# Scale and shift of the first two feature blocks computed by 128 columns at a time, with the token tiles loaded first

## The reference, cut to what matters

```python
c_act = jax.nn.silu(c)                                # (1, 1024)
mod = jnp.dot(c_act, w_ada[l]) + b_ada[l]             # (1, 6 * 1024)
sh_m, sc_m, g_m, sh_f, sc_f, g_f = jnp.split(mod, 6, axis=-1)
h = modulate(rmsnorm(x, norm_mix_g[l]), sh_m, sc_m)   # x_hat * g * (1 + sc_m) + sh_m, (512, 1024)
z = jnp.einsum('bsd,de->bse', h, w_in[l])             # (512, 5 * 1024): u, v, pool, two gates
...
```

## Time and profile before

| | |
|---|---|
| median of 3 runs | 770.53 us (768.27 to 771.75) |
| the profiled execution, its own time | 770.69 us |
| its span in the profile | 768.8 us |
| mean granted TensorE clock | 0.995 |
| PE busy / DVE busy / ACT busy | 97% / 78% / 51% of the span |
| DMA | 187 MB, mean 243 GB/s |

### The profile page before, as it was taken

One profiled execution on the slowest core, in us unless ns is written; L12 is line 12 of the kernel. 1 busy time (PEld: TensorE's weight loads), 2 busy tenths in 40 slices (PEclk: granted clock), 3 DMA queues, 4 the chain that ended last, 5 costly groups with the idle time before them and its releaser, 6 DMA issues.

```text
span 768.8 us, 10951 instructions
## 1 busy us (share of the span) xinstructions
PE 743.4 (97%) x3500; PEld 612.6 (80%) x3501; DVE 599.6 (78%) x824; ACT 392.2 (51%) x360; POOL 195.8 (25%) x80
## 2 busy tenths in 40 slices
PE   7899999999999999999999899999999999999995
PEld 6788888776888888887788587888888888888884
DVE  4894426764674765758768899999999999999985
ACT  4546333324232231324345267777777777777744
POOL 1000004102000000000064111555555555555533
PEclk9999999999999999999999999999999999999999
DMA  8989414211375563917472818899999999999895
GB/s 299 318 271 389 151 55 147 72 56 57 109 267 170 167 215 123 313 55 273 170 265 85 318 44 294 308 370 393 365 366 364 363 358 384 373 369 374 313 187 168
DMA packets 108709, 187.18 MB, mean 243 GB/s; under 512 B 7096, under 2 KB 58360, under 8 KB 108685
## 3 DMA queue, kind: packets, MB, share of 16 engines
q1 hardware_dynamic: 101276, 173.58, 62.7%
q0 software_dynamic: 5792, 11.65, 5.6%
q10 hardware_dynamic: 1616, 1.65, 0.6%
HBM read 180.47 MB, written 15.73 MB: 255 GB/s over the span
## 4 chain that ended last, share of the span: by engine, by line
PE 85%; DVE 8%; DMA 3%; issue 1%; ACT 1%; SPq 1%; DVEq 0%; POOLq 0%; ACTq 0%
PE ps L1522 25%; PE ps L1523 25%; PE ps L1524 25%; DVE wsplit L843 3%; PE ps L1782 2%; DMA raw<-in_w_ada 2%; PE ps L1886 1%; PE ps L1652 1%; DVE raw L932 1%; PE ps L1713 1%; DMA raw<-in_w_out 1%; DMA work<-hf_rows,tok_idx 1%; PE ps L1818 1%; PE ps L1772 1%; DVE raw L886 1%
## 5 line engine op out<-in xcount | busy, mean ns | idle before, releaser
L843 DVE TENSOR_TENSOR wsplit<-raw,wsplit 128x2048 fp32r<-128x2048 f32 x128 | 289.8, 2289 | 57.0 <-ACT wsplit L565 34.2
L752 ACT ACTIVATE wsplit<-raw 128x2048 fp32r<-128x2048 f32 x96 | 183.8, 1921 | 69.4 <-PE ps L1524 69.4
L512 POOL DMA_INDIRECT expert_rows<-work,dest_now x14 | 106.8, 7628 | 105.2 <-DVE work L1402 97.3
L1522 PE MATMUL ps<-wsplit,hgT 128*128 128x512 f32 x264 | 104.5, 396 | 1.3 <-DVE hgT L1313 1.3
L1524 PE MATMUL ps<-wsplit,hgT 128*128 128x512 f32 x264 | 103.1, 390 | 0.0
L1523 PE MATMUL ps<-wsplit,hgT 128*128 128x512 f32 x264 | 102.9, 390 | 0.0
L1522 PE MATMUL ps<-hT,wsplit 128*128 128x512 f32 x256 | 101.1, 395 | 1.0 <-DVE mx L1028 1.0
L1524 PE MATMUL ps<-hT,wsplit 128*128 128x512 f32 x256 | 99.7, 390 | 0.0
L1523 PE MATMUL ps<-hT,wsplit 128*128 128x512 f32 x256 | 99.7, 390 | 0.0
L886 DVE SCALAR_TENSOR_TENSOR raw<-raw,c_silu 128x256 f32 (+1 forms) x128 | 62.0, 485 | 12.6 <-DMA raw<-in_w_ada 8.6
L520 POOL TENSOR_TENSOR wsplit<-raw,wsplit 128x2048 fp32r<-128x2048 f32 x2 | 9.2, 4614 | 198.3 <-ACT wsplit L565 198.2
(11 more groups left out here) (299 smaller groups left out, 1278.3 us busy)
## 6 DMA issues: line engine op xcount, KB each, us to landing
raw<-in_w_exp_gate SPq DMA_DIRECT2D x32, 1024.0 KB
raw<-in_w_exp_up SPq DMA_DIRECT2D x32, 1024.0 KB
raw<-in_w_exp_down SPq DMA_DIRECT2D x32, 1024.0 KB
raw<-in_w_in SPq DMA_DIRECT2D x20, 1024.0 KB
raw<-in_w_ada SPq DMA_DIRECT2D x16, 1024.0 KB
raw<-in_w_ada SPq DMA_DIRECT2D x16, 512.0 KB, 5.9
expert_rows<-tmp SPq DMA_DIRECT2D x4, 1024.0 KB, 11.4
raw<-in_w_branch_a SPq DMA_DIRECT2D x4, 1024.0 KB
```

The source lines that it names most:

```text
L512: g.indirect_dma_start(out=y_dram, out_offset=bass.IndirectOffsetOnAxis(ap=dest_now[:, 0:1], axis=0), in_=y, in_offset=None, bounds_check= ...
L752: A_(wsplit[:, c, 0, :], raw[:, c, :], ACT.Copy).then_inc(hi_ready, 1)
L843: V.tensor_tensor(wsplit[:, n, 1, :], raw[:, slot, :], wsplit[:, n, 0, :].bitcast(F32), ALU.subtract).then_inc(lo_ready, 1)
L1522: nc.tensor.matmul(out, w_hi, m_hi_, start=first, stop=False)
```

## The change

- **Loads.** The four tiles of x come first. Behind them come, for the first feature block, its 128 columns of shift and 128 of scale over all 1024 rows (`load_eighth(0)`, two DMAs of 0.52 MB in runs of 512 bytes, each with its own semaphore), then the rows of `w_in` for that block (0.52 MB), then the same for the second block. All that follows is loaded as before, but for the waits, whose events now come at other times: `load_ada(3)` waits for the first `first_modulation`, `load_v(1)` for the second.
- **First block.** PE sums the eight row groups of the shift columns by itself, as products of the piece of `w_ada` with a column of c_silu (line 1602 of the new kernel), and four of the eight of the scale columns; DVE sums the other four (975, 977), which PE adds (1608). `first_modulation(0)` makes gain and shift of it.
- **Second block.** DVE sums all eight row groups, 256 columns at a time (1026, 1028); PE sums them over the partitions (1676) behind its first row of V products, and `first_modulation(1)` follows.
- **ACT** makes the high parts of the first V weights in two halves (615), scales no token tile any more, treats block 0 and block 1 apart (`h_block`), and copies block 1 out of PSUM as well. DVE scales all four tiles.
- **PE** makes the transposes of the fourth tile in pieces between the columns, the first V group is (0, 0) instead of (0, 1), and `mod_columns(1)` stands one group later.

The sum over rows is done in another order, so results differ by rounding.

The diff, cut to its core:

```diff
-V_FIRST = ((0, 1), (1, 1), (2, 1), (2, 0), (3, 0), (0, 0), (1, 0))
+V_FIRST = ((0, 0), (0, 1), (1, 1), (2, 1), (2, 0), (3, 0), (1, 0))
...
+            def load_eighth(e):
+
+                chunk = raw[:, ADA_PLACE[e], :].rearrange("p (k s n) -> p k s n", k=ND, s=2)
+                for part, landing in ((0, ada_in[e]), (1, scale_in[e])):
+                    sp.dma_start(chunk[:, :, part, :],
+                                 shift_scale[:, :, part, e * P:(e + 1) * P]).then_inc(landing, 16)
...
-            load_x(0)
-            load_x(1)
-            load_ada(0)
-            load_x(2)
-            load_x(3)
-            load_ada(1)
-            load_v(0)
+            for t in range(NT):
+                load_x(t)
+            load_eighth(0)
+            load_first_v(0, value_in)
+            load_eighth(1)
+            load_first_v(1, landed[V_PLACE[0]])
...
+            def h_block(k):
+
+                if k >= 1:
+                    act.wait_ge(xT_saved, 4)
+                A_(x_block(k), x_block(k), ACT.Identity, scale=gain[:, k:k + 1],
+                   bias=mod_cols[:, k:k + 1]).then_inc(h_aff, 1)
+                act.wait_ge(h_aff, k + 1)
+                A_(hT[:, 0, k, :], x_block(k), ACT.Copy).then_inc(h_hi, 1)
...
+            act.wait_ge(value_in, 16)
+            first_v_hi(0).then_inc(value_hi, 1)
             act.wait_ge(xT_t, NT)
...
+            act.wait_ge(gain_ready, 1)
+            h_block(0)
+            act.wait_ge(xT_t, NT + 1)
+            x_saved(4, 6)
+            act.wait_ge(xT_t, NT + 2)
+            x_saved(6, 8)
+            x_saved(2, 4)
+            act.wait_ge(xT_t, NT + 3)
+            x_saved(1, 2)
+            act.wait_ge(landed[V_PLACE[0]], 16)
+            first_v_hi(1).then_inc(hi_ready, 1)
+            act.wait_ge(gain_ready, 2)
+            h_block(1)
...
+            def block_sums(e, part, rows):
+
+                acc = macc_a[:, 0, e * P:(e + 1) * P]
+                for k in rows:
+                    w_k = raw[:, ADA_PLACE[e], (2 * k + part) * P:(2 * k + part + 1) * P]
...
+            for t in range(NT):
+                x_inverse(t)
+            dve.wait_ge(scale_in[0], 16)
+            block_sums(0, 1, range(4, ND))
+            first_modulation(0)
+            dve.wait_ge(value_hi, 1)
+            v_lo(0, 0)
+            h_low(0)
...
+            dve.wait_ge(ada_in[1], 16)
+            dve.wait_ge(scale_in[1], 16)
+            both = macc_a[:, 0, P:3 * P]
+            for k in range(ND):
+                w_k = raw[:, ADA_PLACE[1], 2 * k * P:(2 * k + 2) * P]
...
+            ins.then_inc(block_sum, 1)
+            dve.wait_ge(hi_ready, 1)
+            v_lo(0, 1)
+            first_modulation(1)
+            ada_head(2, range(2))
             h_low(1)
...
-                ada_head(2 * q, range(4) if q == 1 else range(1, 4))
+                ada_head(2 * q, range(2 if q == 1 else 1, 4))
...
             pe.wait_ge(cols_ready, 1)
-            for t in range(NT):
-                idle_products((12, 3, 16, 0)[t], 3, 3 * P)
...
+            for t in range(NT - 1):
+                idle_products((10, 3, 3)[t], 3, 3 * P)
+                pe.wait_ge(xhat_ready, t + 1)
...
+            idle_products(3, 3, 3 * P)
+            pe.wait_ge(c_ready, 1)
+            pe.wait_ge(ada_in[0], 16)
+            first_columns(0, 0, range(ND))
+            pe.wait_ge(xhat_ready, NT)
+            turn_x(3, 0).then_inc(xT_t, 1)
+            pe.wait_ge(scale_in[0], 16)
+            first_columns(0, 1, range(4))
+            summed_column(0, 1, False)
+            for k in range(2, 7):
+                mm = turn_x(3, k)
+            mm.then_inc(xT_t, 1)
+            pe.wait_ge(gain_ready, 1)
+            turn_x(3, 7).then_inc(xT_t, 1)
+            idle_products(7, 1, 3 * P)
+            turn_x(3, 1).then_inc(xT_t, 1)
...
-                    if k == 1 and i == 4:
+                    if k == 0 and i in (1, 3, 4, 6):
+                        pe.wait_ge(xT_saved, (1, 3, 4, 6).index(i) + 1)
+                    if i == 5 and k == 1:
                         mod_columns(1)
                     v_block(0, k, t, half)
+                if k == 0:
+                    pe.wait_ge(block_sum, 2)
...
+                    mm.then_inc(mod_mm, 1)
```

138 lines of the change are left out of this document (69 added, 69 removed).

## The result

The change makes the kernel slower by a little: 772.47 us median (770.44 to 774.25, 20 runs) against 770.38 (768.27 to 772.64, 20 runs), a ratio of 1.0029 with a 95% interval of 1.0019 to 1.0039. The forecast was 770.2 with a range of 767.8 to 773.0. The time lies in the range and within 0.5% of the kernel before, but the difference of 2.1 us is clear of the interval, and it points the other way: the forecast's sum left T where it was and took 0.3 us off behind it.

A forecast was written before the change was run, and what follows sets the result against it. PE, busy 97% of the span, bounds the kernel, so only its early idle time or unneeded products could be saved. T unchanged, then -0.3 us from 770.69 gives 770.4; the runs' median lies 0.16 lower: 770.2, range 767.8 to 773.0.

The forecast's parts named there:

- T: End of DVE's sums for the second quarter (ada_head(3)), which release mod_columns(1) on PE; 33.30 us in the first profile.
- 0.3 us off behind it: Between T and the second quarter: PE starts at T + 3.8, held by block 2's low part, instead of T + 4.2.
- T "33.3, as before": End of DVE's second-quarter sums: DVE's saving is taken up by 3.95 us of sums, a second modulation and waits.
- The surplus of the slow start: First w_ada load: 2.5 us beyond full rate, counted once for the first eighth, possible from 0 to 5 us.
- rival 1: Loads in 512-byte runs land late, at the scale and second-eighth waits: up to +2.2 us, 772.7; up to +3.8 0.13.
- Rival 4: Eighths in 512-byte runs load at the full 386 GB/s, 2.7 us each: T near 32.8, 769.7 us; chance 0.08.
- Rival 2: PE's clock falls in the V rows: second row +0.2 us, first row +1.4 us, 771.9; chance 0.09.
- the first V product near 20.6: Start of PE's first V row: 20.6 us instead of 24.89, 4.3 us earlier.
- the new wait ahead of the second row: PE idle between first and second V rows, 25.9 to 28.65 us: 2.75 us, ended by DVE's low part of block 1.
- DVE's sums for the second block: Eight DVE sums of 256 columns once the second eighth has landed: 3.95 us, to 24.8.
- the 4 us: Naive reading: the first V product moves some 4 us earlier and the end with it; the forecast rejected the second half.
- T's weight of one for one: At the end of DVE's second-quarter sums: each microsecond of landing beyond 16.05 moves that date one for one.

The follow-up runs named there:

- the filled runs: Three versions of the change with both rows' gaps filled: as such 770.85 us, without products between the columns 770.71, with column sums inside the first row 771.09.
- the filled run: The change with the first block's scale summed on DVE and unread PE products filling the gaps ahead of both V rows: 770.85 us, 1.0012.
- the bare columns: The filled run without the four unread products among the shift's one-column products: 770.71 us, 1.0023.
- the scale on DVE: The change with the first block's scale sums all on DVE and 6 unread PE products in place of its 4 scale columns: 771.09 us, 1.0022.
- the eighth early: The change with the first eighth of w_ada loaded ahead of token tiles 2 and 3: 777.58 us, 1.0098.
- one gap filled: The change with 8 unread PE products ahead of the second row of V products: 771.89 us, 1.0028.
- the sums inside: The filled run with the second block's column sums inside the first row and DVE's low half behind the gain: 771.09 us, 1.0008.
- the run with GpSimd: The filled run with GpSimd making the second low half of V weights, column sums inside the first row, gain directly behind DVE's sums: 772.43 us, 1.0034.

## Why the prediction was wrong, step by step

- **T "33.3, as before" is the step that failed, and it failed on its second half.** The changed kernel's own T is 33.8, 34.8 and 35.9 in its three profiles, each with a slow stretch ahead of the first row; in the filled runs, where there is none, it is 32.84, 33.01 and 33.04, a little under the forecast. The kernel before was the wrong part. Its T is 31.02 and 31.20 in two further profiles, and 33.22 where the loads started slowly. So at full clock the change puts T 1.8 us later, where the sum had nothing. The sum was made against one execution, in which the largest thing the change removes, DVE's wait of 2.27 us for `w_ada`, was about 2 us larger than in the two others. The time of that execution (770.69) did not give this away, because it had no slow stretch ahead of the gather, and the third profile of before, with T 2.0 us earlier, took 770.14.
- **Where the chain is longer.** DVE is busy 19.32 us of the 21.35 up to T in the second profile of before, and 19.77 of 23.17 in the filled run (rows below). The filled run does four more sums on DVE than the change itself. The work grew by 0.45 us, the idle time by 1.4. Its named waits are 1.18 us before (0.18 for `w_ada`, 0.69 for PE's columns, 0.31 for ACT) and 2.14 in the filled run: 1.06 and 0.35 for PE's two column sums, 0.37 and 0.36 for ACT's two blocks. At full clock this was 1.4 us of time (1.0 with the bare columns). The prediction counted these waits one by one for the new kernel, but set their sum against one old T.

The stretch up to T, of the second profile of before and of the filled run:

```profile
9.67:31.02 21.35, 20.23 (x129) 18.25 (x127) 19.32 (x36) 11.30 (x15) 0.00 (x0) 0.92 1.00 372
```

```profile
9.67:32.84 23.17, 21.36 (x147) 18.85 (x145) 19.77 (x46) 12.08 (x17) 0.00 (x0) 1.00 0.93 314
```

- **The surplus of the slow start** was put down to `w_ada`, as 0 to twice 2.5 us. It goes with what is loaded first: in the change the token tiles had it. ACT waited for the third until 10.50 and the fourth landed at 11.72 (forecast: both in by 10.2), while the eighth had landed at 14.73 instead of 16.05, so rival 1 (late eighths) did not occur. That some of the 16 DMA engines start more slowly than others is in no row: rows 6 give their mean share, 0.88.
- **Runs of 512 bytes** moved 335 to 348 GB/s (12 to 15 us above); I had taken 313 from the nearest row and 386, the rate of runs of 1 KB, as the upper end. Rival 4, the full rate, did not come. The rule of the Trainium skill named there (DMA: Bandwidth & Descriptors, Specifications) is not borne out here: 335 to 348 is short of 386. But this term did not matter: other waits were behind it.
- **Rival 2, the clock, came true and was mis-sized.** I gave it a chance of 0.09 and prices of 0.2 us for the second row and 1.4 for the first. The second row had 6.8 us at 1.2 GHz, not 3.4. PE reached `mod_columns(1)` 1.8 us after T and got to the second quarter at T + 5.6 instead of T + 3.8. The first row was hit as well. That the gap of 2.75 us (measured 2.83) could do what one of 3.07 did was written down and given too little weight; it did so in all three profiles of the change and in that with the scale on DVE, and not in that with the eighth early. Filling both gaps took 1.0029 to 1.0012.
- **Right:** the first V product near 20.6 (20.63 and 20.11 where the clock held), the new wait ahead of the second row, DVE's sums for the second block (forecast 3.95, measured 3.90 from 20.90 to 24.80), that almost nothing of the 4 us counts, and T's weight of one for one. `load_v(1)` was in time, if barely: its high part ended at 34.67, and DVE asked at 34.77.

Together: compared with the runs of the kernel before in its own group, both at .994 or more, the versions of the change lose: 1.4 us with both rows filled, 1.3 each with one gap filled and with the scale on DVE, 1.0 with the bare columns, 0.9 with the sums inside (4 to 12 runs each; the run with GpSimd has one such run and that with the eighth early none). So the chain costs 0.9 to 1.4 us. The change itself has only three runs at .994 or more, with a median of 770.92; that is 1.5 us above the 769.41 of before, and its clock adds 1.6 us (770.92 to 772.47). The kernel before loses to its clock too: 0.5 us by all of its 97 runs (769.41 to a median of 769.87), 1.0 against the 770.38 of the result's own group, whose clocks are not known run by run. 1.5 + 1.6 less 0.5 to 1.0 is 2.1 to 2.6, and 2.1 were measured. This splits the difference by definition and is good to half a microsecond at best: the medians of the kernel before differ by up to 1.7 us from group to group, and the fillers cost about half a microsecond themselves. Not settled is why the loads start slowly in some executions, and why the mean clock is below .994 in 56 of the 97 runs of the kernel before.

## What to carry to other kernels

Before costing a change against a wait for a load, profile the unchanged kernel two or three times: here the wait was 2.3 us in one execution (770.69 us in all) and nothing in two others (768.15 and 770.14). Splitting a block in two saves the first product's time only if nothing on the way to the next common date gets a round trip more; add up the waits of the chain, not only its work. And a new gap on PE can be paid twice, once as idle time and again in the products behind it: here one or two slow stretches followed it in four profiles of five.

## What the runs showed of the hardware

- With PE at rest for 2.8 us ahead of the second row, its clock was at half behind it in every profile of the change and in the one with the scale on DVE, for 3.4 to 6.8 us; with the eighth early the same rest (2.83 us) left it at full over 37.1 to 40.5 us. With 8 unread products behind 0.59 us of rest it was at full. After 3.72 us of rest it stayed at half for 13.7 us though PE was busy for 12.71 of them, with transposes, column products and unread products.
- Runs with a mean clock below .994 are longer by 1.1 us in the kernel before (770.54 against 769.41) and by 1.7 us in the change (772.62 against 770.92). So the clock goes with a good part of a kernel's spread from run to run.
- One GpSimd subtraction of 2.36 us (128x1024, both inputs in SBUF) held VectorE's sums up by 2.20 us.
- The rate of the first loads differs by execution: 343 and 388 GB/s over 6 to 12 us in two profiles of the same kernel.
